# A new order of the merged stage, two of its sparse steps divided, and products of ones at its borders

## The reference

```python
def layer_step(x, pos, nsa_fn, shift_prev, wkv_prev, conv_prev, lp):
    h = rms_norm(x, lp["norm_mix_pre"])
    proj = h @ lp["w_in"]
    q, kv_rows, win_rows, gates = nsa_project(proj[..., :NSA_PROJ], pos)
    o_nsa, win_state = nsa_fn(q, kv_rows, win_rows, gates)
    o_rwkv, shift_new, wkv_new = rwkv_time_mix(proj[..., NSA_PROJ:], shift_prev, wkv_prev, lp)
    mixed = jnp.concatenate([o_nsa.astype(x.dtype), o_rwkv.astype(x.dtype)], axis=-1) @ lp["w_out"]
    x = x + rms_norm(mixed, lp["norm_mix_post"])
    f, conv_new = conv_ffn(rms_norm(x, lp["norm_ffn_pre"]), conv_prev, lp)
    x = x + rms_norm(f, lp["norm_ffn_post"])
    return x, kv_rows, win_state, wkv_new, shift_new, conv_new
```

## Time and profile before

| | |
|---|---|
| median of 3 runs | 2032.62 us (2030.53 to 2034.79) |
| the profiled execution | 2032.35 us |
| its span, first to last instruction | 2030.5 us |
| mean granted clock of TensorE | 0.976 |
| TensorE, busy | 1946.6 us (96%) |
| VectorE, busy | 1238.5 us (61%) |
| ScalarE, busy | 731.8 us (36%) |
| merged stage, layer 0 | 172.5 to 560.6 us |
| merged stage, layer 1 | 1178.4 to 1562.4 us |

### The profile page before, as it was taken

The page is one execution under the profiler, slowest core; times in us unless marked ns, Lnnn a source line. Parts: engine busy times, 40 slices in busy tenths (PEclk is TensorE's granted clock), DMA queues, the critical chain, the costliest instruction groups (busy, mean ns, idle before and its releaser), DMA issues.

```text
span 2030.5 us, 53402 instructions
## 1 busy us (share of the span) xinstructions
PE 1946.6 (96%) x22468; PEld 1808.9 (89%) x22468; DVE 1238.5 (61%) x2066; ACT 731.8 (36%) x1394; POOL 30.0 (1%) x143
## 2 busy tenths in 40 slices
PE   7999999998999999999999999999998999999997
PEld 7998888776798999999999988887677999999997
DVE  3475767778637666552255767687876376655423
ACT  3222443644534222232232224445545342222321
POOL 0000000000000000000000000000000000000000
PEclk9998899999999999999999988999998999999999
DMA  5325434143421322333332254432433222222332
GB/s 214 93 74 163 145 118 145 49 127 90 128 79 64 94 89 90 94 95 104 100 140 84 73 181 130 134 116 72 132 106 93 80 73 94 94 88 91 97 101 88
DMA packets 152721, 214.27 MB, mean 106 GB/s; under 512 B 18465, under 2 KB 118306, under 8 KB 150818
## 3 DMA queue, kind: packets, MB, share of 16 engines
q1 hardware_dynamic: 133762, 200.38, 31.4%
q10 hardware_dynamic: 18720, 10.49, 1.7%
HBM read 202.58 MB, written 16.59 MB: 108 GB/s over the span
## 4 chain that ended last, share of the span: by engine, by line
PE 73%; DVE 17%; ACT 4%; issue 2%; DMA 1%; ACTq 1%; SPq 0%; DVEq 0%
PE ps L884 18%; PE ps L886 18%; PE ps L885 18%; PE ps L1271 3%; DVE arena L2144 1%; DVE arena L2135 1%; DVE arena L2097 1%; PE ps L1242 1%; PE ps L905 1%; DVE arena L1935 1%; PE ps L1235 1%; PE ps L906 1%; PE ps L943 1%; PE ps L1138 1%; PE ps L1256 1%
## 5 line engine op out<-in xcount | busy, mean ns | idle before, releaser
L886 PE MATMUL ps<-hm_hi,ring_lo 128*128 128x260 f32 x1568 | 446.7, 285 | 0.0
L1826 DVE TENSOR_TENSOR ring_lo<-ring,ring_hi 128x1024 fp32r<-128x1024 f32 x135 | 165.4, 1225 | 308.2 <-ACT ring_hi L1429 306.6
L884 PE MATMUL ps<-hm_hi,ring_hi 128*128 128x260 f32 x1056 | 302.1, 286 | 6.8 <-DVE hm_lo L1833 4.6
L885 PE MATMUL ps<-hm_lo,ring_hi 128*128 128x260 f32 x1056 | 300.8, 285 | 0.0
L886 PEld LDWEIGHTS ps<-hm_hi,ring_lo 128*128 128x128 f32 x1568 | 299.1, 191 | 0.0
L1429 ACT ACTIVATE ring_hi<-ring 128x1024 fp32r<-128x1024 f32 x135 | 142.9, 1060 | 321.6 <-DMA ring<-in_w 316.1
L884 PEld LDWEIGHTS ps<-hm_hi,ring_hi 128*128 128x128 f32 x1056 | 201.7, 191 | 9.6 <-issue 9.6
L885 PEld LDWEIGHTS ps<-hm_lo,ring_hi 128*128 128x128 f32 x1056 | 201.6, 191 | 0.0
L886 PE MATMUL ps<-hf_hi,ring_lo 128*128 128x260 f32 x704 | 198.9, 283 | 0.0
L886 PE MATMUL ps<-in_hi,ring_lo 128*128 128x260 f32 x704 | 198.8, 282 | 0.0
L1826 DVE TENSOR_TENSOR ring_lo<-ring,extra_hi 128x1024 fp32r<-128x1024 f32 x67 | 82.1, 1225 | 159.7 <-ACT extra_hi L1429 158.9
(11 more groups left out here) (432 smaller groups left out, 4391.0 us busy)
## 6 DMA issues: line engine op xcount, KB each, us to landing
ring<-in_w SPq DMA_DIRECT2D x202, 512.0 KB, 3.6
extra<-in_kv_cmp SPq DMA_DIRECT2D x96, 128.0 KB, 2.2
arena<-in_kv_cmp SPq DMA_DIRECT2D x80, 128.0 KB, 2.3
slot<-in_kv_cmp SPq DMA_DIRECT2D x80, 128.0 KB, 2.7
out_win_old<-in_win SPq DMA_DIRECT2D x16, 511.0 KB, 4.3
arena<-in_k_sel SPq DMA_DIRECT2D x72, 64.0 KB, 2.0
extra<-in_k_sel SPq DMA_DIRECT2D x72, 64.0 KB, 1.9
slot<-in_v_sel SPq DMA_DIRECT2D x72, 64.0 KB, 2.0
```

The source lines that it names most:

```text
L884: mmul(out, wh, hi[:, k, cols], start=(k == 0), stop=False)
L885: mmul(out, wh, lo[:, k, cols], start=False, stop=False)
L886: last = mmul(out, wl, hi[:, k, cols], start=False, stop=(ci == len(chunks) - 1 and k == k1 - 1))
L1826: v.tensor_tensor(w_low(l, n), ring[:, (N_CHUNK * l + n) % RING, :], w_high(l, n), SUB).then_inc(S["w_lo"], 1)
```

## The change

1. `ORDER` is another string (hexadecimal digits now, as there is a tenth thread).
2. `read` is divided into four steps of 16 products (`("read", 0)` to `("read", 3)`), which can stand apart; only the first waits for `add` and only the last tells VectorE. `c_imp` is divided into two (each one product for the block scores and the sums of four samples).
3. `turn_over(4)`: four products of ones of 128x128 behind the input projection's last tile, ahead of the waits for the last evacuations.
4. A new thread `warm` of three steps, each one product of ones with 512 columns into bank 4, free once the last attention unit is evacuated.

The diff, without the bodies of the two strings:

```diff
--- before.py
+++ after.py
@@ -66,6 +66,7 @@
 N_CHUNK = C_DOWN + 3 * KB
 RING = 3
 FRONT = 3
+WARM = 3
 KEEP = 5
 
 
@@ -244,7 +245,7 @@
             ("squares", "DVE", 0.5), ("tanh", "ACT", 2.0), ("small", "PE", 2.6, "tanh", "squares"), ("sig", "ACT", 2.2, "small"),
             ("root", "ACT", 0.4, "small"), ("prep", "DVE", 5.6, "sig", "root"), ("pin", "ACT", 0.4, "sig"), ("rk", "PE", 0.3, "prep"),
             ("rks", "DVE", 0.3, "rk"), ("left", "PE", 4.0, "rks"), ("scaled", "DVE", 2.4, "left"), ("right", "PE", 4.0, "scaled"),
-            ("decay", "DVE", 4.7, "pin", "scaled"), ("add", "DVE", 4.7, "right"), ("read", "PE", 4.0, "add"), ("yc", "DVE", 0.4, "read"),
+            ("decay", "DVE", 4.7, "pin", "scaled"), ("add", "DVE", 4.7, "right"), *((("read", j), "PE", 1.05, "add") for j in range(RJ)), ("yc", "DVE", 0.4, ("read", RJ - 1)),
             ("mean", "PE", 0.3, "yc"), ("msub", "DVE", 0.6, "mean"), ("var", "PE", 0.3, "msub"), ("vrec", "DVE", 0.9, "var"),
             ("vroot", "ACT", 0.4, "vrec"), ("out", "DVE", 1.4, "vroot"), ("store", "ACT", 1.0, "out")):
         out.append((("rs", 0, name), engine, us, [("rs", 0, a) for a in after]))
@@ -301,8 +302,11 @@
                                  ("cmp_h", "DVE", 0.57), ("cmp_out", "PE", 0.7), ("cmp_keep", "DVE", 0.63)):
             put(name, b, engine, us)
     for name, engine, us in (("c_scores", "PE", 1.6), ("c_max", "DVE", 0.44), ("c_exp", "ACT", 0.6), ("c_weigh", "DVE", 1.0),
-                             ("c_same", "PE", 0.8), ("c_impt", "DVE", 0.8), ("c_imp", "PE", 2.6), ("c_top", "DVE", 3.9)):
+                             ("c_same", "PE", 0.8), ("c_impt", "DVE", 0.8)):
         put(name, 0, engine, us)
+    for h in range(2):
+        put("c_imp", h, "PE", 1.3)
+    put("c_top", 0, "DVE", 3.9)
     for h in range(2):
         put("win_new", h, "DVE", 0.3, U_WK + h)
         put("win_k", h, "PE", 1.05, U_WK + h)
@@ -365,22 +369,27 @@
     return [(("early", 0, "whi"), "ACT", 1.15, [("smp", 6, "sel_v")]), (("early", 0, "wlo"), "DVE", 1.4, [("early", 0, "whi")])]
 
 
-ORDER = ("700890878970970708817888789708007880778787077810808887887898877011187077170817107181900008188198107881808882877338238322"
...
+def warm_thread(att):
+
+    return [(("warm", i, "ones"), "PE", 0.9, [att[-2][0]]) for i in range(WARM)]
+
+
+ORDER = ("007898870790887090818787978870000878887788870117088809707870180178081797810170088771108890701801170887107827893888782732"
...
 
 
 def merged_order():
 
-    smp = sample_thread()
-    rows = (step_thread(), *rwkv_threads(), early_thread(), page_thread(smp), att_thread(), smp, load_thread(smp))
+    smp, att = sample_thread(), att_thread()
+    rows = (step_thread(), *rwkv_threads(), early_thread(), page_thread(smp), att, smp, load_thread(smp), warm_thread(att))
     at, order = [0] * len(rows), []
     for c in ORDER:
-        i = int(c)
+        i = int(c, 16)
         key = rows[i][at[i]][0]
         at[i] += 1
         if key[0] != "load":
@@ -1008,6 +1017,7 @@
                     dense_tile([(m, 0, KB)], in_hi, in_lo)
                     if m > NT:
                         beside(m - NT - 1)
+                turn_over(4)
                 pe.wait_ge(S["evac_a"], N_IN)
                 pe.wait_ge(S["evac_v"], N_IN)
                 pe.wait_ge(S["kcp_ok"], 1)
@@ -1061,13 +1071,15 @@
                                     last = mmul(ps[r, j, b * CH:(b + 1) * CH],
                                                 pr[r, 2 * RJ + j, SEQ + b:SEQ + b + 1].to_broadcast((HD, HD)), eye[r, :], start=True, stop=True)
                         last.then_inc(S["rs_mm"], 1)
-                    elif stage == "read":
-                        pe.wait_ge(S["rs_prep"], 4)
-                        for j in range(RJ):
-                            for b in range(DEC):
-                                for r in HP:
-                                    last = mmul(ps[r, 0, j * DEC + b:j * DEC + b + 1], ss[r, j, b, :], pr[r, j, SEQ + b:SEQ + b + 1], start=True, stop=True)
-                        last.then_inc(S["rs_mm"], 1)
+                    elif stage[0] == "read":
+                        j = stage[1]
+                        if j == 0:
+                            pe.wait_ge(S["rs_prep"], 4)
+                        for b in range(DEC):
+                            for r in HP:
+                                last = mmul(ps[r, 0, j * DEC + b:j * DEC + b + 1], ss[r, j, b, :], pr[r, j, SEQ + b:SEQ + b + 1], start=True, stop=True)
+                        if j == RJ - 1:
+                            last.then_inc(S["rs_mm"], 1)
                     elif stage == "mean":
                         pe.wait_ge(S["rs_prep"], 5)
                         mmul(ps[:, 1, 0:RJ * DEC], onesblk[:], kk_s, start=True, stop=True).then_inc(S["rs_mm"], 1)
@@ -1286,12 +1298,13 @@
                         mmul(W[0:NCS, 0:ROWS], pcs[0:ROWS, 0:NCS], K("same", ROWS), start=True, stop=True)
                         nc.tensor.transpose(W[0:NCS, ROWS:2 * ROWS], pcg[0:ROWS, 0:NCS], ident[0:ROWS, 0:ROWS]).then_inc(S["ss_mm"], 1)
                     elif step == "c_imp":
-                        pe.wait_ge(S["ss_v"], V_AT["c_impt"])
-                        for h in range(2):
-                            mmul(W[:, h * NSEL:(h + 1) * NSEL], impt[0:NCS, h, :, :].rearrange("p j r -> p (j r)"), K("hit", NCS), start=True, stop=True)
-                        for b in range(DEC):
+                        if n == 0:
+                            pe.wait_ge(S["ss_v"], V_AT["c_impt"])
+                        mmul(W[:, n * NSEL:(n + 1) * NSEL], impt[0:NCS, n, :, :].rearrange("p j r -> p (j r)"), K("hit", NCS), start=True, stop=True)
+                        for b in range(QD * n, QD * (n + 1)):
                             last = mmul(W[:, P + b * HEADS:P + (b + 1) * HEADS], vcs[0:NCS, b, :], pct[0:NCS, b * HEADS:(b + 1) * HEADS], start=True, stop=True)
-                        last.then_inc(S["ss_mm"], 1)
+                        if n == 1:
+                            last.then_inc(S["ss_mm"], 1)
                     elif step == "win_k":
                         pe.wait_ge(S["kw_new"], n + 1)
                         if n == 0:
@@ -1365,6 +1378,9 @@
                         sample(step, n)
                     elif side == "rs":
                         one_step(step)
+                    elif side == "warm":
+                        pe.wait_ge(S["pt_ev"], len(UNITS))
+                        mmul(ps[:, 4, :], ones[:], K("scan"), start=True, stop=True)
                     elif side == "pages":
                         pass
                     else:
@@ -1705,6 +1721,8 @@
                         sample(step, n)
                     elif side == "rs":
                         one_step(step)
+                    elif side == "warm":
+                        pass
                     elif side == "pages":
                         load_unit(act, mybir.EngineType.Activation, l, n, lo=PAGES - ACT_PAGES)
                     elif side == "early":
@@ -2295,7 +2313,7 @@
                         sample(step, n)
                     elif side == "rs":
                         one_step(step)
-                    elif side == "pages":
+                    elif side in ("pages", "warm"):
                         pass
                     elif side == "early":
                         if step == "wlo":
```

More of the change, by code:

```diff
@@ new lines @@
+ORDER = ("007898870790887090818787978870000878887788870117088809707870180178081797810170088771108890701801170887107827893888782732"
+         "322382732278838238723778822371717838178789283878172888227388281272727889287272172827877781827829787288782881878822198288"
+         "978778277298827718128782217822182292187287797287878272488278487738428278847222284828822874883773428383278327977382238782"
+         "378287827798197812277831288337772877877182281728721879162887129721817227187282828172228221882282871287226487792887394422"
+         "747886877672422273623228293279223392724478237732927726173723712728637172277277112712177171821721218127271827767972288282"
+         "279872228282827287827789427822878746886222887782622227227897234328797247672824736872287372823776762279227872737232423279"
+         "72272724272772223232732736722747478949748357748875a488a7a84")
```

## The result

The changed kernel takes **2041.38 us** (median of 10 runs, 2033.25 to 2048.07) against 2032.61 of the kernel before beside it: a ratio of **1.0043 [1.0029, 1.0057]**, slower. The prediction was 2019 and faster. The profiled execution took 2042.15 us with a span of 2040.3, 9.8 longer than before. One run of all that follow, of 2118.02 us at a mean clock of 0.842, was in a slow state and is left out.

What follows compares the result with a forecast made beforehand. TensorE, 73% of the chain, was taken to bound the kernel through idle time and low clock. Per layer -5.0 + 3.1 + 3.1 + 2.85 + 2.8 = 6.85, twice 13.7, off 2032.35: 2019 us; 8-in-10 range 2004 to 2037.

Steps and rivals of the forecast that it cites:

- part 2: Merged stage's head: chunks ahead of `small` wait for the pair weights, so `left` starts later; 5.0 us lost a layer.
- Part 3: VectorE's order behind `left`: `mask1` and `weigh1` moved behind `add`, so `add` ends earlier; 3.1 us gained a layer.
- Part 4: `read` divided into four pieces between chunks: the clock stays up; net 3.1 us gained a layer, 2.7 lost otherwise.
- part 5: `c_same` and `c_imp`: two waits go (1.35) and half the dip's worth returns (1.5); 2.85 us gained a layer.
- part 6: Tail: 2.8 us gained a layer, 0.9 from the new order and 1.9 from `warm` holding the projection's clock.
- Part 7: Rest of the merged stage: remaining waits come from VectorE's queues; no change taken, 7 us either way.
- Part 1: Eight records of ones at the stage's head: the wait ahead of `cs0` covers their 1.0 us; 0 gained or lost.
- The low case: At the head, the clock stays low through `small` after the first two chunks; `left` 5.0 us later.
- other end: At the head, the clock rises at 185.75 as before, so `left` starts only 1.05 us later.
- The head isn't made up: Rival: the head's wait costs 5.0 a layer, dips at `read` and `c_imp` stay; slower, 2037 us, chance 0.15.
- VectorE takes the gain back: Rival: in the last 177 us TensorE waits longer for VectorE, only the tail's gain is left; 2027 us, chance 0.15.

Runs made afterwards that it cites:

- the new first half alone: Changed kernel's first 409 steps (`small` ahead of first chunks, chunks (1,6), (1,7) ahead of `read`), then kernel before's order, with products of ones: 2026.86 us, 0.9967.
- both ends mended: Changed kernel with `small` ahead of the first chunks and, from the last recurrence piece's second `ucopy`, kernel before's order with four products of ones: 2032.02 us, 0.9988.

## Why the prediction was wrong, step by step

The forecast had the head's loss right and five gains against it; of these only the products of ones show in a time. Per layer, predicted against measured in one execution of each kernel (table above, layer 0 / layer 1, a gain positive). A gain of 6.85 was forecast for each layer; the measured rows add up to losses of 1.3 and 7.7:

| step | predicted | measured |
|---|---|---|
| part 2, head | -5.0 | -5.5 / -6.1 |
| parts 3 and 4, to `pairb` | +6.2 | +0.8 / -0.7 |
| part 5, to unit 12 | +2.85 | +3.9 / +3.7 |
| parts 6 and 7, to the projection | +0.9 | -2.0 / -6.1 |
| part 6, the clock behind it | +1.9 | +1.5 / +1.5 |

**Part 1, right.** The eight records took 1.05 and the wait for `cs0` shrank from 1.14 to 0.25; leaving them out changed nothing that shows.

**Part 2, right, near the end taken.** The wait was 6.67 (6.3 predicted), the first two chunks 3.78 (3.6), `small` 4.8 (5.0), all low, and `left` came 5.5 later behind `cs0`. The low case held: two chunks didn't raise the clock for `small`. Some of that was luck, as layer 1 of the old order with chunks first met the rise of the clock that the step had named as its other end. The Trainium skill's rule ("TensorE: Matmul & The Clock Gate", Part 2, on weight loads) that matmuls keep program order is borne out by the row: `small`, which waits for no weights, starts at 185.86, behind the chunks that did.

**Part 3, right but not on the path.** `add` ends 17.1 behind the start of `left` (16.6 predicted, 19.7 before). But `lora_w` starts only 1.6 earlier, and the work that made room for it, two chunks (1.16 us each, at 220.34 and 222.45), now stands behind it.

**Part 4, the first step that failed.** It took the dip for a property of `read` in one run. Divided, three pieces run at the full clock and the fourth doesn't:

```profile
218.22 1.09 PE L1080 MATMUL ps<-arena 64*64 64x1 f32 x32 [0.41 <-DVEq L442]
...
227.38 1.87 PE L1080 MATMUL ps<-arena 64*64 64x1 f32 x32
```

In every profile of this study, and in both layers, the clock falls 0.3 to 11.4 us behind the start of `read`, be it whole or in pieces; only layer 1 of the run with ones among the pieces is without that. The dip lasts 6.8 to 20.5 us there, and the same order has met both. The step had an open end ("if the dip stays, 2.7 lost"); together with part 3 that end gives 3.1 - 2.7 = 0.4, and 0.8 and -0.7 were measured, or -0.2 and -1.7 with `tm 0` counted alike. What sets the fall there stays open.

**Part 5, right in sum, wrong in mechanism.** The waits of 0.69 and 0.66 are gone. The 6.9 us dip only came apart, into two of 3.4:

```profile
378.40:381.80 3.40, 3.40 (x65) 3.40 (x64) 2.67 (x18) 0.81 (x1) 0.00 (x0) 0.51 0.02 5
402.30:405.70 3.40, 3.40 (x40) 2.62 (x38) 1.83 (x8) 1.99 (x3) 0.00 (x0) 0.51 0.02 5
```

The stretch gained 3.9, of which less idle time makes 1.6 (4.2 to 2.6), and one of the two dips has moved into the next stretch. The gain isn't steady either: the kernel with the new first half alone takes 145.97 and 148.35 us here, the old order with products of ones 148.81 and 147.51, and it is no faster.

**Part 6, wrong in sign for the order, right for the clock.** It saw that `out` would end last, and still counted `scores23` 2.3 earlier as a gain. In layer 0 `scores23` starts 153.1 behind unit 12's scores, 153.7 before: 0.6. In layer 1 it is 155.9, 151.5 before: 4.5 later. And the reciprocal ends 10.7 behind the end of `scores23` (10.3 predicted), the projection starts 17.7 behind it instead of 16.4: of the 1.3 missing, 0.9 lie behind `vrec`. The waits of 1.84 and 1.16 us, put down to `weigh23` standing behind `vrec`, held up the end only because `turn23` and `values23` then ran low: ScalarE's `heads` (second row) ended last, 0.9 us behind VectorE's `out` (first row). With products of ones in the old order `heads` (third row) ends 0.3 ahead of `out`:

```profile
557.37 0.69 DVE L2104 TENSOR_TENSOR hm<-arena 128x512 f32<-128x512 f32 x1
558.40 0.60 ACT L1653 ACTIVATE hm<-ps 128x512 f32<-128x512 f32 x1 [2.12 <-PE ps L1256]
```
```profile
556.30 0.60 ACT L1668 ACTIVATE hm<-ps 128x512 f32<-128x512 f32 x1 [1.25 <-PE ps L1268]
556.48 0.69 DVE L2121 TENSOR_TENSOR hm<-arena 128x512 f32<-128x512 f32 x1
```

So an earlier `weigh` had nothing left to gain once the clock held, and by itself it made the end 1.5 later a layer. In the changed kernel `vrec` doesn't even wait for `weigh`, but for TensorE's `var`, which now stands with `mean` behind `scores23`, `yout` and `values22`:

```profile
552.97 0.69 DVE L2113 TENSOR_SCALAR arena<-ps 128x512 f32<-128x512 f32 x1 [0.57 <-PE ps L1221]
```

The clock's part held: products of ones alone are worth 6.7 in two layers where they fill most of the waits.

**Part 7, wrong.** "I take no change" rested on the remaining waits being VectorE's. The new order brought a wait for a transfer, at `sel_v 3`, 1.4 and 2.2 us. Part 7 counted distances in products; this one needed the time that SyncE's and ScalarE's queues take to issue a unit's 16 pages (in layer 0 of the kernel after, SyncE's 12 from 496.77 to 504.78 and ScalarE's 4 from 504.34 to 506.18; `sel_v 3` starts at 509.31). Between the scores of units 12 and 23 of layer 1 TensorE idles 12.1 us instead of 8.3, with 4.7 of it in the two waits for pages, 0.6 before.

**The rivals.** "The head isn't made up" had the right sign and the nearest time, 2037, but not the reason: by its own rule parts 3 to 5 returned more than 2.2 in layer 0 (4.7, or 3.5 with `inv 5` and `win_max_b` counted alike) and about as much in layer 1 (3.0, or 1.8), and what decided was the last 170 us, which "VectorE takes the gain back" had named, at nothing instead of a loss. Each rival took one failure; two came together, and the range ended at 2037, short of 2041.

## What to carry to other kernels

In a stage bound by one engine, first ask of each step moved forward what it waits for and which thread is queued behind it: one step ahead of a transfer cost 8 us here, more than all the reordering returned. Before an elementwise engine's order is changed at a stage's end, find out which result ends last, and whether it does so only because products ahead of it ran low: filling the busiest engine's waits with dummy products gave 6.7 us with the old order untouched. And don't count on a dip of the clock going away because the work in it was spread.

## What the hardware showed that I had not expected

TensorE's granted clock fell to 0.51, its lower level, in stretches in which the engine was busy without a gap (20.50 of 20.50 us above), and dense 128x128 products in them stayed low. Nor did a long wait stand ahead of that fall: in the kernel with `small` first, TensorE was busy at the full clock in 9.79 of the 10.2 us before.

```profile
204.00:214.20 10.20, 9.79 (x196) 9.05 (x193) 9.87 (x6) 0.89 (x4) 0.00 (x0) 1.00 0.53 154
```

And equal instruction streams don't meet equal dips: in the kernel with both ends mended, `read` and what surrounds it met 20.5 low us in layer 0 and, in layer 1, a full clock up to 1227.5 and then 6.8:

```profile
213.70:234.20 20.50, 20.50 (x164) 17.24 (x163) 9.23 (x25) 11.98 (x37) 0.00 (x0) 0.51 0.33 96
1227.50:1234.30 6.80, 6.04 (x22) 4.71 (x23) 4.62 (x16) 5.42 (x16) 0.00 (x0) 0.52 0.07 24
```

That kernel's runs lie between 2021.33 and 2035.26, those of the old order with products of ones between 2024.18 and 2028.19. The difference of 14 us from one run to the next is as large as what was to be measured, which is why some of these comparisons stay open. That the dips make this difference is not shown, as each kernel has one trace.
